# A two-block transformer kernel on one Trainium2 core: the second mixer's stages in another order on every engine

## The reference, cut to what matters

```python
h = modulate(rmsnorm_2(x, g_mix[l]), sh1, sc1)
proj = h @ w_in[l]            # 3*512 rkv, 512 xb, 512 gb, 1024 gate a, 1024 gate b
# rwkv7_time_mix
rkv = rkv + (token_shift(rkv) - rkv) * mu_rkv;  r, k, v = jnp.split(rkv, 3, axis=-1)
dx = token_shift(xn) - xn;  xw, xa, xg = (xn + dx * mu_wag[i] for i in range(3))
w_log = -softplus(-(w0 + jnp.tanh(xw @ w1) @ w2)) - 0.5
decay = exp(-exp(w_log));  a = sigmoid(a0 + (xa @ a1) @ a2);  g = sigmoid(xg @ g1) @ g2
kk = heads(k * k_k);  kk = kk * rsqrt(sum(kk * kk) + 1e-12);  k = k * (1 + (a - 1) * k_a)
state = state * w_t + (state @ -kk_t) * (kk*a)_t + v_t * k_t;  y_t = state @ r_t
y = (y - mean) * rsqrt(var + GN_EPS) * lnx_g + lnx_b + sum(r * k * r_k) * v
y_a = y * g
# rglru_branch: conv of xb, two block-diagonal gates, a scan over time
y_b = h_scan * gelu(gb)
merged = sigmoid(gate_a) * (y_a @ p_a) + sigmoid(gate_b) * (y_b @ p_b)
x = x + gt1 * (merged @ w_out)
# then hier_moe: 32 experts of 1024x256, 1024x256 and 256x1024
```

## Time and profile before

| what | before |
|---|---|
| median of 3 runs | 2273.73 us (2266.32 to 2276.39) |
| the profiled execution's own time | 2271.23 us |
| its span in the trace | 2269.7 us |
| PE busy in the span | 2064.4 us, 91% |
| DVE, ACT, POOL busy | 727.6, 294.0, 156.7 us |
| mean granted TensorE clock | 0.963 |
| HBM read | 645.94 MB |
| second mixer, first product to `wo2` | 1606.06 to 1958.82 us |
| second MoE, first to last round | 2022.5 to 2259.8 us |

### The profile page before, as it was taken

One profiled execution on the slowest core, in us unless ns is written; L12 is line 12 of the kernel. 1 busy time (PEld: TensorE's weight loads), 2 busy tenths in 40 slices (PEclk: granted clock), 3 DMA queues, 4 the chain that ended last, 5 costly groups with the idle time before them and its releaser, 6 DMA issues.

```text
span 2269.7 us, 22425 instructions
## 1 busy us (share of the span) xinstructions
PE 2064.4 (91%) x9478; PEld 1089.3 (48%) x9478; DVE 727.6 (32%) x1223; ACT 294.0 (13%) x643; POOL 156.7 (7%) x207
## 2 busy tenths in 40 slices
PE   3989999999999999999899999998889798779997
PEld 1644468855453333333333333333667697453332
DVE  2266858243221111111111111111363552441223
ACT  1111130121020000000000000000122211020000
POOL 3022420010000000000000000000200100010100
PEclk7999999999999999999999999999899997889999
DMA  7698720233659999999999999999432301539995
GB/s 288 235 370 332 278 75 22 70 107 121 229 232 379 428 427 428 427 427 429 427 427 427 427 429 426 428 428 398 131 111 75 111 1 56 207 139 421 420 422 216
DMA packets 91992, 648.59 MB, mean 286 GB/s; under 512 B 10032, under 2 KB 15384, under 8 KB 47568
## 3 DMA queue, kind: packets, MB, share of 16 engines
q1 hardware_dynamic: 87216, 640.41, 68.8%
q0 software_dynamic: 4672, 6.68, 1.0%
HBM read 645.94 MB, written 1.11 MB: 285 GB/s over the span
## 4 chain that ended last, share of the span: by engine, by line
PE 77%; DMA 15%; DVE 4%; issue 2%; ACT 2%; POOL 0%; SPq 0%; POOLq 0%; DVEq 0%; ACTq 0%
PE ps L218 35%; PE ps L1661 14%; DMA sb<-in_w_down 7%; PE ps L1688 7%; DMA sb<-in_w_gate_up 5%; PE ps L2477 5%; PE ps L1404 5%; PE ps L2501 3%; PE ps L1650 2%; PE ps L223 2%; PE ps L604 2%; DMA sb<-in_w_in 1%; PE ps L621 1%; DVE sb L973 1%; PE ps L659 0%
## 5 line engine op out<-in xcount | busy, mean ns | idle before, releaser
L218 PE MATMUL ps<-sb 128*128 128x128 f32 (+4 forms) x3846 | 863.0, 389 | 84.9 <-DVE sb L2376 12.3
L218 PEld LDWEIGHTS ps<-sb 128*128 128x128 f32 (+1 forms) x3846 | 605.2, 198 | 329.9 <-issue 238.9
L1661 PE MATMUL ps<-sb 128*64 128x512 f32 x2048 | 448.2, 594 | 1.2 <-DMA sb<-in_w_gate_up 0.8
L1661 PEld LDWEIGHTS ps<-sb 128*64 128x64 f32 x2048 | 143.3, 137 | 303.9 <-issue 291.8
L1688 PE MATMUL ps<-sb 128*64 128x512 f32 x1024 | 234.0, 612 | 49.9 <-DMA sb<-in_w_down 26.9
L1778 DVE TENSOR_SCALAR sb<-ps 128x512 f32<-128x512 f32 x32 | 33.5, 1048 | 488.1 <-PE ps L1661 488.1
L1688 PEld LDWEIGHTS ps<-sb 128*64 128x64 f32 x1024 | 87.5, 140 | 185.4 <-issue 185.4
L1415 DVE TENSOR_TENSOR sb<-ps,sb 128x512 f32<-128x512 f32 x64 | 44.2, 691 | 384.3 <-PE ps L1688 295.1
L1744 ACT COPY sb<-ps 128x512 f32<-128x512 f32 x32 | 18.7, 585 | 786.0 <-PE ps L223 786.0
L1404 PE MATMUL ps<-sb 128*128 128x512 f32 x256 | 115.3, 593 | 1.7 <-DVE sb L1415 1.7
L2477 PE MATMUL ps<-sb 128*64 128x512 f32 x512 | 112.7, 593 | 4.3 <-POOL sb L2574 3.7
(11 more groups left out here) (333 smaller groups left out, 1113.9 us busy)
## 6 DMA issues: line engine op xcount, KB each, us to landing
sb<-in_w_gate_up SPq DMA_DIRECT2D x128, 2048.0 KB, 23.8
sb<-in_w_down SPq DMA_DIRECT2D x64, 2048.0 KB, 26.2
sb<-in_w_in SPq DMA_DIRECT2D x24, 2048.0 KB, 8.3
sb<-in_w1e SPq DMA_DIRECT2D x32, 1024.0 KB, 15.0
sb<-in_w3e SPq DMA_DIRECT2D x32, 1024.0 KB, 17.1
sb<-in_w2e SPq DMA_DIRECT2D x32, 1024.0 KB, 19.7
sb<-in_w_ada SPq DMA_DIRECT2D x24, 1024.0 KB, 8.4
sb<-in_w_mod SPq DMA_DIRECT2D x16, 1024.0 KB, 12.4
```

The source lines that it names most:

```text
L218: last = te.matmul(o, l, r, start=i == 0, stop=i == len(pairs) - 1)
L1661: last = te.matmul(ps[64 * h:64 * h + 64, 512 * c:512 * c + 512], xg[k][:, t, 64 * m:64 * m + 64], w[:, at:at + 512], start=False, stop=t ...
```

## The change

The tiles, the matmuls and the weights are the same, but their order is another, and PSUM banks are dealt in the new order.

- PE: the first low-rank product follows `xb`; each later `lo` and `lw` stands behind a feature product. `raw 1` (the keys) comes before `raw 0`, and `kk` stands after the first tile of `raw 0`. `gate 0` and `gate 1` follow `raw 2`; the four tiles of `gate 2` stand behind the four groups of pair matrices; the four of `gate 3` are cut in halves of four matmuls (`half_gate`), one half before or behind every step of the chain `x`, `u`, `s`, `y`, `m1`. `pb 0` stands before `m2`, the other seven behind `cb`, ahead of `pa`.
- DVE: the mixed inputs, the convolution and the recurrence follow in the order in which PE needs them. `N`, `W` and `Ti` are written before the pair matrices. The gain and the gate (`lnx_g`, `gT`) and the bias and bonus are multiplied out beforehand, so that behind the reciprocal only a product and a sum are left, in two halves; the reciprocal and ACT's square root are cut in halves too.
- New tiles `lora`, `spare` and `keys` take the place of storage that was shared.
- SP: `w_out` no longer goes through `r3` but into slots 3 and 4 (`r_out`), after `y 1`; the expert weights follow in slots 5, 6, 1, 0, 2, 3, 4. `p_a` waits for the last tile of `gate 3`.

```diff
-        mix2 = [("h3", t) for t in range(8)] + [("xb", f) for f in range(4)] + [("gb", f) for f in range(4)]
...
+        mix2 = [("h3", t) for t in range(8)] + [("xb", f) for f in range(4)] + [("lo", 0)] + [("gb", f) for f in range(4)]
...
+        r_out = SlotTable(slots, r3.after(), ids=(3, 4))
...
+            feat2(weights(next(order), r3), [("raw", 1, f) for f in range(4)])
+            lora_out(1)
+            lora_in(2)
+            w = weights(next(order), r3)
+            feat2(w, [("raw", 0, 0)])
             te.wait_ge(s["kq"], 1)
-            heads_sum("kk", ex)
...
+            heads_sum("kk", keys)
+            feat2(w, [("raw", 0, f) for f in (1, 2, 3)])
+            lora_out(2)
+            feat2(weights(next(order), r3), [("raw", 2, f) for f in range(4)])
+            for k in range(2):
+                feat2(weights(next(order), r3), [("gate", k, f) for f in range(4)])
...
                 last.then_inc(is_full(("nn", g)), 1)
+                feat2(w, [("gate", 2, g)])
...
+            def half_gate(f, part):
+                o = P(("gate", 3, f)) if part else opened(("gate", 3, f))
+                for t in range(4 * part, 4 * part + 4):
+                    last = te.matmul(o[:, 0:256], w[:, t, 128 * f:128 * f + 128], hv[:, t, :], start=t == 0, stop=t == 7)
+                if part:
+                    last.then_inc(is_full(("gate", 3, f)), 1)
+
+            half_gate(0, 0)
...
+            product_b(0)
             te.wait_ge(s["yq"], 1)
             heads_sum("m2", yT3)
             te.wait_ge(s["wr2"], 64)
             router_constant(1, 36)
+            for j in range(1, 8):
+                product_b(j)
             te.wait_ge(s["ya"], 1)
...
             ac.wait_ge(*read_at(("kk", 2)))
-            ac.activation(cumx, cumx, ACT.Sqrt).then_inc(s["kn"], 1)
-            scalar_gate(2)
+            ac.activation(spare, spare, ACT.Sqrt).then_inc(s["kn"], 1)
+            scalar_copies([("raw", 0, f) for f in range(3)], raw[0], 1)
             ac.wait_ge(s["sc0"], 1)
             ac.activation(sc01, sc01, ACT.Exp).then_inc(s["sc1"], 1)
             scalar_exps(lw, cum, 1.0, nmid)
             scalar_exps(ex, cum, -1.0, mid)
             scalar_exps(cumx, cumx, 1.0, nmid)
...
+            o = filled(ac, ("raw", 0, 3))
+            ac.copy(raw[0][:, 3, 1:257], o[:, 0:256]).then_inc(is_read(("raw", 0, 3)), 1)
...
-            ve.wait_ge(s["sd"], 1)
-            ve.reciprocal(sd, sd).then_inc(dv.up(), 1)
-            settle()
-            ve.tensor_tensor(yq, yq, sd, MUL).then_inc(dv.up(), 1)
...
+            gated_b(0)
+            router_weights(1, 36)
+            gated_b(1)
+            for f in (0, 2):
+                fs = slice(f, f + 2)
+                ve.wait_ge(s["sd"], f // 2 + 1)
+                ve.reciprocal(sd[:, fs, :], sd[:, fs, :]).then_inc(dv.up(), 1)
+                settle()
+                ve.tensor_tensor(yq[:, fs, :], yq[:, fs, :], sd[:, fs, :], MUL).then_inc(dv.up(), 1)
+                settle()
+                ve.tensor_tensor(rT[:, fs, :], yq[:, fs, :], kT3[:, fs, :], ADD).then_inc(s["ya"] if f else dv.up(), 1)
+            for j in range(2, 8):
+                gated_b(j)
...
-        r4 = SlotTable(slots, r3.after(), parts=2, ids=(3, 4, 5, 6, 2, 1, 0))
+        r4 = SlotTable(slots, r_out.after(), parts=2, ids=(5, 6, 1, 0, 2, 3, 4))
...
+            sp.wait_ge(*full_at(("y", 1)))
+            for c in range(2):
+                load(c, r_out)
```

More of the change, by code:

```diff
@@ L1840, in build @@
         w2s, a2s, g2s = P4.take(512), P4.take(512), P4.take(512)
+        lora = P4.take(256)
+        spare = P4.take(4, 256)
+        keys = xb[:, :, 0:256]
         rg = Arena(sb, ar0, d0)
@@ L1912, in sync_mix2 @@
         def sync_mix2():
-            for n in range(12):
+            for n in range(len(r3.loads)):
                 if n < 2:
@@ L1919, in tensor_mix2, with feat2 @@
             order = iter(range(len(r3.loads)))
-            def feat2(names):
-                w = weights(next(order), r3)
+            def feat2(w, names):
                 for name in names:
@@ L1939, in tensor_mix2 @@
             te.wait_ge(*read_at(("h3", 7)))
-            feat2([("xb", f) for f in range(4)])
-            feat2([("gb", f) for f in range(4)])
-            feat2([("raw", 0, f) for f in range(4)])
+            feat2(weights(next(order), r3), [("xb", f) for f in range(4)])
+            te.wait_ge(s["lora_w"], 96)
+            lora_in(0)
+            feat2(weights(next(order), r3), [("gb", f) for f in range(4)])
+            lora_out(0)
+            lora_in(1)
             te.wait_ge(s["xc"], 1)
@@ L2052, in tensor_mix2, with product_b @@
                 last.then_inc(is_full(("y", c)), 1)
+            half_gate(3, 0)
             te.wait_ge(*read_at(("y", 1)))
             heads_sum("m1", yT3)
+            half_gate(3, 1)
+            wb = weights(next(order), r3)
+            def product_b(j):
+                o = opened(("pb", j))
+                mm(o[:, 0:256], [(wb[:, k, 128 * j:128 * j + 128], gb[:, k, :]) for k in range(4)]).then_inc(is_full(("pb", j)), 1)
+            product_b(0)
             te.wait_ge(s["yq"], 1)
@@ L2068, in tensor_mix2 @@
                     if i == 0:
-                        w[c] = weights(next(order), r3)
+                        w[c] = weights(c, r_out)
                     o = opened(("wo2", c, i))
@@ L2155, in scalar_mix2 @@
                 last.then_inc(is_read(("vt", f)), 1)
+            scalar_gate(2, range(4))
             for l in range(1, 7):
```

321 lines of the change are left out of this document (172 added, 149 removed).

## The result

The changed kernel takes 2203.49 us (median of 4 runs, 2201.19 to 2204.05). The kernel before took 2274.8 us beside it (4 runs, 2266.32 to 2276.39). The ratio is 0.9692, with a 95% interval of 0.9667 to 0.9717. The forecast was 2203 us, and the range 2194 to 2228. The profiled execution took 2203.47 us.

A forecast was written before the change was run, and what follows sets the result against it. PE bounds the kernel, losing time to waits and a low clock. The stretch to `wo2`: 277.5 + 2.3 + 2.7 + 0.5 + 1.0 + 0.8 = 284.8 us, a 68.0 us gain from 2271.2, so 2203 us; range 2194 to 2228.

The forecast's parts named there:

- The clock term: First product to `wo2`: PE runs nearly without waits, so the full clock returns 22.0 of 24.3 us.
- the clock does not come back: Rival, chance 0.11: waits shrink but PE keeps swinging between clock levels as in the chain; gain 46, time 2225 us.
- The waits: First product to `wo2`: PE's 51.0 us of waiting on single DVE and ACT steps mostly goes, by moving work beside them.
- Meeting point 1: Keys' sums, behind `raw 1`: PE has 8.7 us of work, DVE and ACT need 7 to 8; no wait.
- Meeting point 2: Exponentials: PE waits in `raw 2` for the bank ACT frees with its last `raw 0` copy; a new 2.7 us.
- Meeting point 3: Group norm before `pa`: PE's 13.7 us of work ties with DVE and ACT; 0.5 us for the bank of `pa 0`.
- two near ties: Keys' sums and group norm, where cover barely suffices: 0.8 us added, the mean of 0 and some 1.5.
- The pair matrices and the chain: Waits of 16.9 us around the pair matrices and 4.9 in x, u, s, y go, covered by moved work.
- DVE and ACT as the bound of the meeting points: Rival, chance 0.12: late DVE or ACT steps pass delay on; 16 us of the gain are lost, 2219 us.
- SP's queue: Loads of `p_a`, `w_out` and experts arrive in time at 5.0 us per 2 MB; second MoE starts with full slots.
- the slower rival: Chance 0.03: ten 2 MB loads behind the last `gate 3` tile outlast 97 us; at 18 us each, 2286 us.
- Behind `wo2`: From `wo2` to the end nothing is moved: 0 change, the same 311 us as before.

The follow-up runs named there:

- The old order with fillers: The kernel before, order untouched, with useless matmuls of 256 columns put into PE's waits; 2253.19 us, ratio 0.9915.
- The kernel without the folding: The changed kernel with gain, bias, bonus and gate applied behind the reciprocal again, in halves; 2205.16 us, ratio 0.9704.

## Why the prediction was right, point by point

**What bounds it.** Right: PE is the bound, and waits and clock were the two losses. The predicted stretch was 284.8 us; it is 281.4, and 279.0 with the better start.

**The clock term** was 22.0 us; 22.4 came back. The old order with fillers gives 19.4 for it without the start, which the prediction had left out of the return. The estimate "busy time times (1 less its clock)" was good to 3 us. The rival "the clock does not come back" is excluded for this order and shown for another: with `gate 3` as a block, waits of 0.68 held the chain at 0.72. The rule of the Trainium skill that stood beside this rival ("TensorE: Matmul & The Clock Gate", "A second HAM failure mode: psum-queue depth-cycling") agrees with that block (0.72) and with the chain of before (0.65), less so with the pair matrices, where waits of 1.29 to 2.57 us left 0.97; it did not bear on the changed kernel, whose groups have no idle time between them.

**The waits** were to fall from 51.0 to 5.0 us and fell to 2.0. These 3.0 us are mis-sized terms, all on the cautious side:

- Meeting point 1 had "1 us to spare". It had about 2.9. From the last `raw 1` tile (ACT's copy begins at 1665.54) to `kq` (L2388 ends at 1671.32) it takes 5.8 us, where I had 7 to 8; PE has 8.7 us of work there, as I had it.
- Meeting point 2 was named with its releaser, ACT's last copy of `raw 0`, at 2.7 us; it is 1.01. My sum from `kq` on, 21.2 us, has terms that add up to 20.9; it measures 21.46 (1671.32 to 1692.78), and it is that near only because 2.3 us of DVE beside POOL's clearing, which I did not see, stand against some 2 us that I had put too high elsewhere. That is luck. The difference in the wait comes from the earlier `kq`.
- Meeting point 3 was called a tie, with 0.5 us for the bank of `pa 0`. It is one: `ya` comes at 1874.25 and PE ends `pb` at 1874.7, so nothing is waited for. DVE's half reciprocals took 3.35 and 3.34 (taken as 3.28). The kernel without the folding shows how close it is: with 3.0 us more work on DVE the wait is 3.0, so nothing was to spare.
- The allowance of 0.8 for two near ties was not needed. Before `wo2` there is 0.97, as said.

**The pair matrices and the chain.** Both covers work as said: taking them off brings back 6.4 us of waits with `gate 2`, and 3.7 us of waits with `gate 3`. What the prediction did not say is that the cover of small waits is worth more in clock than in waits, 8.05 against 3.7 in the chain. It carried both in two sums over the whole stretch, so the total came out right.

**DVE and ACT as the bound of the meeting points.** Not seen. `p_b` ahead of the chain shows what that would look like: 10.1 us before `pa`.

**SP's queue.** It cost nothing, and six more loads cost nothing. The mechanism of the slower rival is real: with sixteen loads between `p_a` and the experts, 28 us are lost. By the rival's own reckoning all seven expert loads had to be there by the MoE's start; that gives 98.4 + 7 x 5.0 = 133 us against the 95.8 between `p_a` and the MoE, so 38 us late. Measured were 28, half as a late start and half in the rounds. It turns between 54 and 98 us from `p_a` to the first expert load; the change has 4. A load of the rival's 16.5 us was not seen: in both kernels SP's loads moved some 375 GB/s.

**Behind `wo2`** I had put 0; it was +1.6 us. The row of the MoE's first round answers for it: 15.65 us where the kernel before took 13.95. The same matmuls take 13.96 with fillers ahead of them, when PE waits 1.11 us and not 3.7. But of the eleven profiles with that wait, two have 13.95 (the kernel before, and the one without the folding), seven 15.65 (the old order with fillers is one), and two 16.5, so what decides it stays open.

**The total.** 68.0 us of gain were forecast on the stretch and 71.4 came; 3.9 us went to a later start of the mixer and the slower first round, neither of which goes with the change: the repeats began the mixer anywhere from 1604.3 to 1609.2, and both lengths of the round occur in either order. That 2203 was hit within 0.5 us is luck: the 3.4 us that the stretch gained beyond the forecast and these 3.9 us nearly cancel, and the changed kernel's own medians run from 2197 to 2203.

## What to carry to other kernels

Read each stage as two losses: its length less PE's busy time, and its busy time times the missing clock. Work that depends on nothing can be cut into pieces at least as long as the waits and put between the steps of a dependent chain; here pieces of 1.73 us over waits of 0.68 returned all of 11.75 us, and useless matmuls 7.4 of them. Before counting a moved instruction as free, look at what the other engines do at that time, and at what would be late next.

## What the runs showed of the hardware

- A DVE pass over 128x1024 from one input took 0.68 us alone and 3.00 beside POOL's clearing of 128x4096 (3.51 us, from 1676.74 to 1680.25): it ended 0.55 us after the clearing did. The clearing beside a reciprocal of 6.54 us slowed neither. The Trainium skill, "SBUF — State Buffer", section "Who interferes with whom", says that a `tensor_scalar` in a 2-port mode and a GpSimd instruction lock each other out for a whole instruction. The trace agrees as far as the pass goes; no run shows in which mode it ran, and the clearing itself took 3.51 us in either place.
- One useless matmul in each of five waits of 0.68 us kept the granted clock of the chain at 1.00, where it was 0.72 without. Four waits of 1.29 to 2.57 us around the pair matrices left it at 0.97.
- The same code behind the same wait of 8.1 us began at 0.93 in 5 of 12 profiles (the kernel before is one of the 5) and at 1.00 in the others, a difference of 2.35 us. With six useless matmuls in that wait, and 3.9 us of it left behind them, one profile began at 1.00 and one at 0.93, so what decides it stays open.
